# Two-block transformer kernel: expert scores in 512-column products, solve masks earlier, odd-layer value and output weights in column halves

## The reference

```python
h  = rms_norm(x, ffn_norm_g)                # block 1 ends in a retrieval layer of
q  = h @ w_peer_query                       # 16384 experts, 8 heads, 16 picks each
idx, g = product_keys_top16(q), softmax(best)
act = gelu(einsum('td,thkd->thk', h, expert_u[idx]))
x  = x + einsum('thk,thkd->td', g * act, expert_v[idx])
# block 2, layer 0: gated delta rule (chunks of 64 tokens)
u, w = solve(a + I, v_beta), solve(a + I, k_beta * exp(gc))   # unit lower triangular
# block 2, layer 1: differential attention, 8 heads, two maps each
q, k, v = split(rms_norm(h) @ w_qkv_o)
p = softmax(q0 k0 + alibi) - lam * softmax(q1 k1 + alibi)
o = rms_norm(p @ v, sub_gain) * (1 - lam_init)
h = h + o @ w_out_o                          # then an MLP and a gated projection
```

## Time and profile before

| | |
|---|---|
| runs | 1817.62 us median, 1812.16 to 1820.73 |
| profiled execution | 1817.64 us, its span 1815.9 us |
| busy, share of span | PE 1742.5 us (96%), POOL 1038.3 (57%), ACT 926.5 (51%), DVE 916.9 (50%) |
| DMA | 288.23 MB, mean 159 GB/s |
| chain that ended last | PE 88%, DVE 4%, ACT 3%, POOL 2% |
| gated steps | 452.97 to 693.87 us |
| odd-layer attention, values to output | 1497.2 to 1592.9 us |

### The profile page before, as it was taken

The page is one execution under the profiler, slowest core; times in us unless marked ns, Lnnn a source line. Parts: engine busy times, 40 slices in busy tenths (PEclk is TensorE's granted clock), DMA queues, the critical chain, the costliest instruction groups (busy, mean ns, idle before and its releaser), DMA issues.

```text
span 1815.9 us, 32194 instructions
## 1 busy us (share of the span) xinstructions
PE 1742.5 (96%) x10852; PEld 1559.5 (86%) x10852; DVE 916.9 (50%) x1865; ACT 926.5 (51%) x1600; POOL 1038.3 (57%) x542
## 2 busy tenths in 40 slices
PE   7989999999999999999999999889999999799998
PEld 6768899999999998888888887878999787689996
DVE  6563329991777775555555557533111366431113
ACT  5555556666333334544544466425445564455554
POOL 7835768888666664000000077427888894478886
PEclk9989999999999999999999999999999998899999
DMA  6623555555444445565565644115555563155553
GB/s 202 173 77 111 172 182 180 181 183 185 140 140 141 140 141 175 193 196 190 193 195 190 217 152 145 36 47 157 185 186 186 161 188 125 47 159 189 189 186 116
DMA packets 81028, 288.23 MB, mean 159 GB/s; under 512 B 9265, under 2 KB 9265, under 8 KB 80433
## 3 DMA queue, kind: packets, MB, share of 16 engines
q1 hardware_dynamic: 80512, 286.10, 49.2%
q10 hardware_dynamic: 432, 1.05, 0.2%
HBM read 285.01 MB, written 2.10 MB: 158 GB/s over the span
## 4 chain that ended last, share of the span: by engine, by line
PE 88%; DVE 4%; ACT 3%; POOL 2%; issue 2%; DMA 0%; DVEq 0%; ACTq 0%; POOLq 0%
PE acc L616 14%; PE acc L617 14%; PE acc L618 14%; PE col L653 11%; PE col L654 11%; PE col L655 11%; PE mb L916 3%; POOL w_lo L1742 2%; PE acc L1067 1%; PE mb L690 1%; DVE H_lo L2568 1%; PE col L1067 1%; ACT hT_hi L1266 1%; PE mb L749 0%; ACT w_hi L1242 0%
## 5 line engine op out<-in xcount | busy, mean ns | idle before, releaser
L1742 POOL TENSOR_TENSOR w_lo<-w_raw,w_hi 128x1024 fp32r<-128x1024 f32 (+1 forms) x410 | 976.5, 2400 | 359.2 <-ACT w_hi L1242 358.7
L1242 ACT ACTIVATE w_hi<-w_raw 128x1024 fp32r<-128x1024 f32 (+1 forms) x539 | 565.8, 1053 | 373.3 <-PE acc L618 338.2
L653 PE MATMUL col<-hT_hi,w_hi 128*128 128x256 f32 x1632 | 467.7, 287 | 2.7 <-DVE hT_lo L1958 1.8
L655 PE MATMUL col<-hT_hi,w_lo 128*128 128x256 f32 x1632 | 461.6, 283 | 0.0
L654 PE MATMUL col<-hT_lo,w_hi 128*128 128x256 f32 x1632 | 461.5, 283 | 0.0
L653 PEld LDWEIGHTS col<-hT_hi,w_hi 128*128 128x128 f32 x1632 | 312.4, 191 | 5.8 <-issue 2.2
L654 PEld LDWEIGHTS col<-hT_lo,w_hi 128*128 128x128 f32 x1632 | 312.7, 192 | 2.4
L655 PEld LDWEIGHTS col<-hT_hi,w_lo 128*128 128x128 f32 x1632 | 312.4, 191 | 0.0
L616 PE MATMUL acc<-w_hi,W_hi 128*128 128x512 f32 x512 | 199.2, 389 | 0.0
L617 PE MATMUL acc<-w_lo,W_hi 128*128 128x512 f32 x512 | 199.2, 389 | 0.0
L618 PE MATMUL acc<-w_hi,W_lo 128*128 128x512 f32 x512 | 199.2, 389 | 0.0
(11 more groups left out here) (514 smaller groups left out, 2669.7 us busy)
## 6 DMA issues: line engine op xcount, KB each, us to landing
w_raw<-in_expert_u SPq DMA_DIRECT2D x128, 512.0 KB, 3.4
w_raw<-in_expert_v SPq DMA_DIRECT2D x128, 512.0 KB, 4.3
w_raw<-in_w_mlp SPq DMA_DIRECT2D x128, 512.0 KB, 3.5
w_raw<-in_w_in SPq DMA_DIRECT2D x24, 512.0 KB, 3.9
w_raw<-in_w_qkv_o SPq DMA_DIRECT2D x24, 512.0 KB, 4.2
w_raw<-in_w_query SPq DMA_DIRECT2D x16, 512.0 KB, 3.5
w_raw<-in_w_gate SPq DMA_DIRECT2D x16, 512.0 KB, 3.5
w_raw<-in_w_qkv_e SPq DMA_DIRECT2D x12, 512.0 KB, 4.0
```

The source lines that it names most:

```text
L653: mm(o, wh[:, k, :], hi[:, k, :], start=k == 0, stop=False)
L655: m = mm(o, wl[:, k, :], hi[:, k, :], start=False, stop=k == KD - 1)
L1242: f(w_hi[:, s, 0:w], w_raw[:, s, 0:w], ACT.Copy).then_inc(sem(f"hi{s}"), 1)
L1742: g.tensor_tensor(w_lo[:, s, 0:w], w_raw[:, s, 0:w], w_hi[:, s, 0:w].bitcast(F32), ALU.subtract).then_inc(sem(f"lo{s}"), 1)
```

## The change

It has three independent parts.

1. **Gated steps.** `hT_hi` and `hT_lo` lie side by side in one tile `hT`. `wide_chunk` multiplies `w_hi` with both at once (512 columns), then `w_lo` with `hT_hi` (256 columns) onto the first half: 16 products for 24. The two halves of the bank are added by VectorE (`both_halves`, a TENSOR_REDUCE over pairs) into `sum_ps`, the upper half of the bank that `merge` uses, and ScalarE reads that. `hot` is cut in two, `merge` of a step comes in the step after, and the gate product now waits for the Gelu.
2. **Solve.** L1T and L2T are made at steps 6 and 7, in other buffers; OC one step later.
3. **Odd-layer attention.** The weights of v and of the output come as halves of 512 columns ("pair" chunks: two row blocks in a chunk). The first half of the values stands before and around the query transposes (copied by ScalarE), the second half is spread over the start of the attention and heads 0 to 3 (`values_w(1, k)`), and the outputs are normalised per pair of heads, turned per map and multiplied as they come. VectorE has fewer operations per head, and has the copy of the turned probabilities from ScalarE (`probs1`). The residual is added in quarter blocks.

```diff
+            def wide_chunk(s):
...
+                    pe.wait_ge(sem("u_sum"), s - 1)
...
+                for k in range(KD):
+                    mm(both, wh[:, k, :], hT[:, :, k, :], start=k == 0, stop=k == KD - 1,
+                       skip_group_check=True)
+                    m = mm(both[:, 0, :], wl[:, k, :], hT_hi[:, k, :], start=False,
+                           stop=k == KD - 1, skip_group_check=True)
+                m.then_inc(sem(f"used{slot}"), 1)
...
                 gates(s)
-                u_chunk(s % 4, (HALF + s) // 4)
+                wide_chunk(s)
...
-                used(act, U0 + n)
+                act.wait_ge(sem("u_sum"), s + 1)
...
+            def both_halves(s):
...
+                used(dve, U0 + n)
...
+                v.tensor_reduce(sum_ps[s % 2], col[n % 2][:, :].rearrange("p (a s) -> p s a", a=2),
+                                AX_X, ALU.add).then_inc(sem("u_sum"), 1)
...
+                dve.wait_ge(sem("gelu"), known)
...
             for s in range(STEPS):
+                if s:
+                    both_halves(s - 1)
+                if s + 2 < STEPS:
+                    first_hot(s + 2)
                 apply_gates(s)
+                if s:
+                    merge(s - 1)
                 if s + 2 < STEPS:
-                    hot(s + 2)
-                if s == STEPS - 1:
-                    gated_lo(0, 0, W0_hi, W0_lo)
-                    gated_lo(1, 1, W0_hi, W0_lo)
-                merge(s)
+                    second_hot(s + 2)
+            both_halves(STEPS - 1)
+            gated_lo(0, 0, W0_hi, W0_lo)
+            gated_lo(1, 1, W0_hi, W0_lo)
+            merge(STEPS - 1)
```

```diff
-        L1T = big("L1T", 105, [P, NT, G_H, P])
+        L1T = big("L1T", 57, [P, NT, G_H, P])
...
-        L2T = big("L2T", 113, [P, NT, G_H, P])
+        L2T = big("L2T", 97, [P, NT, G_H, P])
...
-                if s == MIX_AT + 1:
+                if s in (6, 7):
+                    for t in range(NT):
+                        then(v.tensor_tensor(four((L1T, L2T)[s - 6], t), four(aT, t),
+                                             over(masks[:, s - 2, :], [P, 4, P], 1), ALU.mult))
+                if s == MIX_AT + 2:
```

```diff
+            def values_w(n, k):
...
             for h in range(C_H):
                 if h + 2 < C_H:
                     scores1(2 * h + 4)
                     scores1(2 * h + 5)
+                if h < 4:
+                    values_w(1, (2, 4, 6, 7)[h])
                 pe.wait_ge(sem("attn1"), h + 1)
                 causal_fills(h, PR1[:, (2 * h) % 4, :], "aT", "aT_E")
                 if h:
                     head_values1(h - 1)
+                if h < 2:
+                    values_w(1, 2 * h + 3)
+                if h == 6:
+
+                    pe.wait_ge(sem("ev_v1"), upto("ev_v1", 3))
+                    o1_map(0, acc[2])
+                if h == 7:
+                    pe.wait_ge(sem("ev_v1"), upto("ev_v1", 4))
+                    out_w(0, 0)
+                    out_w(0, 1)
+            o1_map(1, mb[0])
             head_values1(C_H - 1)
...
+            pe.wait_ge(sem("masked1"), 2 * C_H)
+            out_w(1, 0)
+            out_w(1, 1)
+            o1_map(2, mb[1])
...
-                for t, (a, b) in enumerate(halves):
-                    i = v.tensor_scalar(p1[:, a:b], p1[:, a:b], sum1[:, 2 * h + 1, t:t + 1], None,
-                                        ALU.mult)
+                for t, (a, b) in enumerate(((0, P), (P, 3 * P))):
+                    i = v.scalar_tensor_tensor(out=p0[:, a:b], in0=p1[:, a:b],
+                                               scalar=sum1[:, 2 * h + 1, t:t + 1], in1=p0[:, a:b],
+                                               op0=ALU.mult, op1=ALU.add)
+                i.then_inc(sem("attn1"), 1)
+                if h == 4:
+                    values_out(1)
+                if h in (5, 7):
+                    heads_out1((h - 5) // 2)
+            o1_lo(0, acc[2])
+            probs1(C_H - 1)
```

More of the change, by code:

```diff
@@ L91 @@
 ROWS_OVER = -(-R_ALL // SEQ)
+OUT_ORDER = [(n, b) for b in range(4) for n in range(2)]
 def chunk_plan():
@@ L127, in chunk_plan @@
         if layer:
-            for n, name in enumerate(("q1", "k1", "v1")):
+            for n, name in enumerate(("q1", "k1")):
                 rows(name, "w_qkv_o", range(KD), n * D, D)
-            rows("out_o", "w_out_o", range(KD), 0, D)
+            first["v1"] = len(plan)
+            plan.extend(("w_qkv_o", "pair", b, 2 * D + 512 * n, D) for n in range(2)
+                        for b in range(KD // 2))
+            first["out_o"] = len(plan)
+            plan.extend(("w_out_o", "pair", b, 512 * n, D) for n, b in OUT_ORDER)
         first[f"mlp{layer}"] = len(plan)
@@ new lines, in out_w @@
+            def out_w(n, k):
+                if k % 2 == 0:
+                    chunk_in(FIRST["out_o"] + OUT_ORDER.index((n, k // 2)))
+                    pe.wait_ge(sem("o1_E"), upto("o1_E", k // 2 + 1))
+                for t in range(NT):
+                    out_part(n, k, t)
+            pe.wait_ge(sem("qk1"), 2)
+            pe.wait_ge(sem("qm_E"), upto("qm_E", 4))
+            key_maps = head_maps(K1)
+            fills("km", key_maps[0:2])
+            values_w(1, 0)
+            pe.wait_ge(sem("km_E"), upto("km_E", 1))
@@ L1664, in _ @@
                 head_squares(("q1", "k1")[m])
[L1665 removed]
+                split_to(FIRST[nxt] + (7 if m == 0 else 5))
                 if m == 0:
@@ L2503, in _ @@
                         y = YIT if result.startswith("YT") else YI
-                        if s in (11, 12):
-                            then(v.tensor_tensor(four(L1T if s == 11 else L2T, t), four(aT, t),
-                                                 over(masks[:, 4 if s == 11 else 5, :], [P, 4, P], 1),
-                                                 ALU.mult))
                         if result.endswith("+"):
@@ new lines, in masked1, with probs1, heads_out1 @@
+                i.then_inc(sem("masked1"), 1)
+            def probs1(h):
+                dve.wait_ge(sem("aT"), upto("aT", h + 1))
+                if h >= 2:
+                    dve.wait_ge(sem("pv1"), h - 1)
+                v.tensor_copy(PT1[:, h % 2, :], mb[h % 2][:, 0:3 * P]).then_inc(sem("aT_E"), 1)
+            def heads_out1(p):
+                dve.wait_ge(sem("o1_r"), upto("o1_r", p + 1))
+                for hh in range(2):
+                    h = 2 * p + hh
+                    for t in range(NT):
@@ L2655, in heads_out1 @@
                         x = v.scalar_tensor_tensor(
-                            out=O1[:, t, c:c + P], in0=acc[2 * t + part][:, h * P:(h + 1) * P],
-                            scalar=sq16[:, i:i + 1], in1=rows[:, R_SG:R_SG + P], op0=ALU.mult,
+                            out=O1[:, t, h * P:(h + 1) * P],
+                            in0=acc[p % 2][:, 256 * hh + t * P:256 * hh + (t + 1) * P],
+                            scalar=sq16[:, 2 * h + t:2 * h + t + 1], in1=sub_gain, op0=ALU.mult,
                             op1=ALU.mult)
-                then(x, "o1")
+                x.then_inc(sem("o1"), 1)
@@ new lines, in _ @@
+                if h == 4:
[4 more added lines that the diff above has]
+            probs1(C_H - 1)
+            heads_out1(2)
+            o1_lo(1, mb[0])
+            heads_out1(3)
+            o1_lo(2, mb[1])
+            o1_lo(3, mb[0])
+            for t in range(NT):
+                for n in range(2):
+                    if t == 0:
+                        dve.wait_ge(sem("out_full"), n + 1)
+                    else:
+                        used(dve, FIRST["out_o"] + OUT_ORDER.index((n, 3)))
+                    c = slice(n * 512, (n + 1) * 512)
+                    v.tensor_tensor(X[:, t, c], (acc[2 + t], col[t])[n][:, :], X[:, t, c],
+                                    ALU.add).then_inc(sem("ev_out_o"), 1)
```

286 lines of the change are left out of this document (187 added, 99 removed).

## The result

The changed kernel takes 1793.18 us (median of four runs, 1789.70 to 1797.04), the one before 1817.59 in the same comparison; the ratio is 0.987, 95% interval 0.984 to 0.990. It is 24.4 us faster; 1791.5 was forecast.

A forecast was written before the change was run, and what follows sets the result against it. TensorE, busy 96% of the span, was taken as the bound: only fewer or shorter products or its few waits give time. Gated steps −5.4, solve −4.9, odd layer −15.8 sum to −26.1: 1817.6 becomes 1791.5 us, range 1782 to 1806.

The forecast's parts named there:

- the −6.7 of the sum: Gated steps: step falls from 3.76 to 3.66 us, gain 0.105 × 64 = 6.7 us, before the loss at the end.
- The sum's price of 0.60: Gated steps: VectorE's new sum over 128 x 512 elements in PSUM takes 0.60 us, bounds 0.38 and 1.2.
- the cover: Gated steps: VectorE's idle time hides the sum; 3.50 of 3.66 us busy, 0.16 left, VectorE sets the step from 0.76.
- The rival case (VectorE becomes the bound): Gated steps: sum costs 1.2 us, step 4.10, +21.8 us; total 1820 us, no change; chance 0.06.
- The slower case: Gated steps: sum costs 1.45 us, step 4.35, +37.8 us; total 1836 us; decides from price 1.31 on; chance 0.05.
- 0.04 + 0.60 + 0.42 + 0.2 for signals = 1.3 us lost once: End of gated steps: `gated_lo` now stands behind the last sum, delaying the expert_v products by 1.3 us once.
- The −6.4 of the path: Solve: OC transposes start 6.4 us earlier, of which 3.9 is TensorE's gap and 1.7 two groups at half clock.
- the mutual hold-up: Solve: moved masks and GpSimd's operations delay each other; UV late by 2.1, TensorE stalls 1.5 us, bounds 0 and 2.2.
- The walk: Odd layer: summed row prices; heads begin at 1519.4, output products at 1550.5, end 1576.5 against 1592.9, −16.4 us.
- the last term, 2.2 us for half clock: Odd layer: TensorE sparse from about 1541 to 1551, so a lower clock costs 2.2 us more, bounds 0.5 and 4.
- The rival that the interleaved products would cost VectorE its turn: Odd-layer attention: VectorE's chain slips behind TensorE in heads 0 to 3; part 3 −8 to −11, 1797 to 1799; chance 0.17.

The follow-up runs named there:

- e1: The changed kernel with the low parts of the first two gated chunks made ahead of VectorE's last sum, not behind it: 1788.84 us, ratio 0.984.
- e5: e1 with VectorE's sum of the halves made twice in each gated step: 1805.63 us, ratio 0.993; gated steps 253.23 us.
- e3: The changed kernel with the gated part undone (24 products of 256 columns, no sum): 1793.37 us, ratio 0.988.
- e2: e1 with the masks L1T and L2T made at solve steps 10 and 11, not 6 and 7: 1790.36 us, ratio 0.986; solve 49.72 us.
- e6: e1 with the second half of v multiplied before the heads, none between them: 1790.24 us, ratio 0.984; odd layer 130.30 us.
- e7: e1 with the evacuation of the first value half behind head 0's probabilities: 1787.65 us, ratio 0.982; odd layer 125.12 us.
- e8: e1 with the copies of the turned probabilities of heads 3 to 6 back on ScalarE: 1787.43 us, ratio 0.983; odd layer 126.52 us.

## Why the prediction was right or wrong

**The total** (1791.5, range 1782 to 1806) held: 1793.18. That it came within 2 us of the centre is luck in part, because errors of opposite sign met; the range would have held without that. By the stages of the profile the three parts give −0.7 − 6.0 − 17.8 = −24.5 us: part 1 is 4.7 worse than forecast, parts 2 and 3 are 3.1 better.

**Part 1, the step.** Right in mechanism, and nearly in size: 3.66 us forecast, 235.79 / 64 = 3.68 in e1, where nothing of the seam is in it. Against 241.06 that is −5.3 us for the −6.7 of the sum. The sum's price of 0.60 was right (0.61). Wrong was the cover: I had 2.90 us of other work of VectorE in a step, and so a limit of 0.76; e5 shows 2.63 and 1.05. The 2.90 had been read from the first start to the last end of a step with waits in it; operations that follow closely overlap by 0.08 us. The rival case (VectorE becomes the bound) lay further off than its text said. At its price of 1.2 it would have cost some (2.63 + 1.2 − 3.76) × 64 = 4.5 us against before and not 21.8, an estimate with the middle step of e5 for all. The slower case needed a step of 4.21, which is a price of 1.58 and not 1.31.

**Part 1, the seam: the step that failed.** "0.04 + 0.60 + 0.42 + 0.2 for signals = 1.3 us lost once". The gap was 2.94 us (689.50 less the 0.12 behind 686.44), since the two low parts took 2.36 us for 0.76; without these 1.60 it is 1.34, so the order of the operations had been priced rightly and the hold-up was the term left out. I had used the hold-up of VectorE by GpSimd in part 2, from rows, and had not asked what GpSimd ran at the seam. Behind it the clock fell, 1.7 us in 24 products (7.17 to 5.47), a term that I had only in part 3. e1 undoes all of it by three lines in another order, and e3 confirms that the part as changed is worth next to nothing.

**Part 2.** The −6.4 of the path was right; against it stood 1.5 for the mutual hold-up, which measured 0.9 on GpSimd's operations and 0.35 on the path (0.23 of waiting, and the slower start behind it). I had let the masks wait for L1844's 1.67 us; they ran beside it at 0.71 each. What is on GpSimd for long is not what holds VectorE: that operation has 128 x 8 elements. e2 shows the other end: beside 128 x 1024 products from SBUF the same masks took 7.0 us.

**Part 3.** The walk was right to the point where the output products begin (53.5 us after the first product of v, 53.3 forecast), and so was the order of bounds: TensorE's in heads 0 to 3, VectorE's after. Mis-sized was the last term, 2.2 us for half clock: the half clock came, PEclk 0.77 from 1530 to 1545, but inside VectorE's heads, where TensorE had time, and was over as the output products began. So −17.8 for −15.8; it helped that the profiled execution has no value product at half clock, where e1 with the same code has nine and takes 2.2 us more. The rival that the interleaved products would cost VectorE its turn did not come: e6 shows the opposite, 3 to 5.5 us for interleaving. No run takes the other terms of this part one by one (the turning beside other work, VectorE's shorter heads, the output products between them).

## What to carry to other kernels

When an operation of VectorE with two SBUF operands is moved, look up what GpSimd runs at the new place, by the size of its operands and not by its duration: here one collision with a 2.4 us w_lo made VectorE's operation 1.4 to 2.2 us longer, and collisions decided the seam, e2 and e7, and e8 too as far as its rows tell. Write out the first and the last turn of a loop as its own term of the sum; the steady step was right to 1%, and the seam took back 4.6 of its 5.3 us. A clock term belongs to the stretch in which it falls: in heads 5 to 7, where VectorE is the bound, the half clock left the start of the output products within 0.2 us of the forecast.
